# Attention scores of a fused two-model block: one VectorE pass with a row minimum in the first stage, masks added by TensorE in the second and third

## What is computed

```python
s_c = einsum('bghqd,bgnd->bghqn', qblk, k_c) * scale + head_bias(rel_c)      # nsa, compressed keys
s_s = einsum('bghqd,bgqkd->bghqk', qblk, k_sel) * scale + bias_s             # nsa, selected keys
s_w = einsum('bghqd,bgkd->bghqk', qblk, k_wb) * scale + head_bias(rel_w)     # nsa, window
p   = softmax(where(mask, s, NEG))
# even, A: s = q.k * d**-0.5, -inf where a key is not among the 64 best or lies ahead of the query
# odd, C and D: s = q.k * scale, -inf where the key lies ahead of the query; scale is 1/8 for C, 96**-0.5 for D
```

## Time and profile before

| | |
|---|---|
| median of 3 runs | 1409.39 us (1406.6 to 1410.95) |
| the profiled execution | 1416.18 us |
| its span, first to last instruction | 1414.4 us |
| instructions | 27164 |
| mean granted clock of TensorE | 0.972 |
| PE busy | 1311.0 us (93%) |
| DVE busy | 887.8 us (63%) |
| ACT busy | 619.9 us (44%) |
| POOL busy | 430.7 us (30%) |

### The profile page before, as it was taken

The page is one execution under the profiler, slowest core; times in us unless marked ns, Lnnn a source line. Parts: engine busy times, 40 slices in busy tenths (PEclk is TensorE's granted clock), DMA queues, the critical chain, the costliest instruction groups (busy, mean ns, idle before and its releaser), DMA issues.

```text
span 1414.4 us, 27164 instructions
## 1 busy us (share of the span) xinstructions
PE 1311.0 (93%) x10699; PEld 1246.9 (88%) x10717; DVE 887.8 (63%) x1232; ACT 619.9 (44%) x926; POOL 430.7 (30%) x195
## 2 busy tenths in 40 slices
PE   5999999999999998999999789899999997699787
PEld 4999998989999998999999557899998996688667
DVE  3685458786444566555456884755456686774695
ACT  3444335344333345344344774543344445334452
POOL 1444442214444423544430342344441003300042
PEclk9999999999999999999998899999999999999989
DMA  6867764666776546666634113666663461434102
GB/s 195 223 207 223 218 190 133 180 179 190 221 222 184 164 151 185 185 203 191 183 120 149 35 35 105 189 205 185 191 195 105 150 204 43 138 120 137 43 30 90
DMA packets 275098, 222.51 MB, mean 157 GB/s; under 512 B 8082, under 2 KB 256422, under 8 KB 274908
## 3 DMA queue, kind: packets, MB, share of 16 engines
q1 hardware_dynamic: 272528, 215.59, 50.2%
q0 software_dynamic: 1344, 4.46, 1.5%
q10 hardware_dynamic: 1164, 1.62, 0.4%
HBM read 216.40 MB, written 4.19 MB: 156 GB/s over the span
## 4 chain that ended last, share of the span: by engine, by line
PE 74%; DVE 13%; ACT 6%; DMA 3%; issue 3%; POOL 1%; ACTq 0%; POOLq 0%; DVEq 0%; SPq 0%
PE psum L675 23%; PE psum L676 22%; PE psum L677 22%; DVE wal L1587 2%; ACT wah L1170 1%; DVE pbuf L1810 1%; ACT hnh L1239 1%; DVE nmx L1812 1%; DVE hnl L1605 1%; DVE wal L1770 1%; DMA raw_a<-in_ffn_w_in 1%; ACT wbh L1177 1%; PE psum L638 1%; POOL wbl L2197 1%; DVE rms L1577 1%
## 5 line engine op out<-in xcount | busy, mean ns | idle before, releaser
L675 PE MATMUL psum<-hnh,wah 128*128 128x256 f32 (+1 forms) x2080 | 591.6, 284 | 33.5 <-DVE hnl L1605 13.5
L676 PE MATMUL psum<-hnl,wah 128*128 128x256 f32 (+1 forms) x2080 | 582.9, 280 | 0.0
L677 PE MATMUL psum<-hnh,wal 128*128 128x256 f32 (+1 forms) x2080 | 582.6, 280 | 0.0
L2197 POOL TENSOR_TENSOR wbl<-raw_b,wbh 128x1024 fp32r<-128x1024 f32 x111 | 361.3, 3256 | 573.3 <-ACT wbh L1177 467.2
L675 PEld LDWEIGHTS psum<-hnh,wah 128*128 128x128 f32 (+1 forms) x2080 | 397.2, 191 | 21.9 <-issue 10.0
L676 PEld LDWEIGHTS psum<-hnl,wah 128*128 128x128 f32 (+1 forms) x2080 | 395.8, 190 | 2.3 <-issue 1.7
L677 PEld LDWEIGHTS psum<-hnh,wal 128*128 128x128 f32 (+1 forms) x2080 | 395.8, 190 | 0.0
L1587 DVE TENSOR_TENSOR wal<-raw_a,wah 128x2048 fp32r<-128x2048 f32 (+1 forms) x129 | 298.1, 2311 | 102.8 <-ACT wah L1170 101.6
L1170 ACT ACTIVATE wah<-raw_a 128x2048 fp32r<-128x2048 f32 (+2 forms) x127 | 238.9, 1884 | 89.8 <-PE psum L677 64.5
L1277 ACT ACTIVATE gate_hid<-tmp 128x256 f32<-128x256 f32 x88 | 36.7, 417 | 427.9 <-DVE tmp L1705 427.9
L675 PE MATMUL psum<-hidh,wbh 128*128 128x256 f32 x768 | 214.3, 279 | 4.1 <-DVE hidl L1641 3.9
(11 more groups left out here) (289 smaller groups left out, 1557.9 us busy)
## 6 DMA issues: line engine op xcount, KB each, us to landing
raw_a<-in_ffn_w_in SPq DMA_DIRECT2D x176, 512.0 KB, 5.1
raw_b<-in_ffn_w_out SPq DMA_DIRECT2D x88, 512.0 KB, 5.0
raw_a<-in_w_in_even SPq DMA_DIRECT2D x15, 1024.0 KB, 5.4
raw_a<-in_conv_w_in SPq DMA_DIRECT2D x24, 512.0 KB, 3.9
raw_a<-in_w_in_odd SPq DMA_DIRECT2D x11, 1024.0 KB, 5.3
raw_a<-in_w_kv SPq DMA_DIRECT2D x6, 1024.0 KB, 6.4
raw_b<-in_conv_w_out SPq DMA_DIRECT2D x8, 512.0 KB, 5.7
raw_a<-in_attn_w_q SPq DMA_DIRECT2D x4, 1024.0 KB, 5.2
```

What stands on the lines that cost most here:

```text
L675: mm(dst, wh, xh, start=start, stop=False)
L676: mm(dst, wh, xl, start=False, stop=False)
L677: return mm(dst, wl, xh, start=False, stop=stop)
L2197: g.tensor_tensor(wbl[:, s], raw_b[:, s], wbh[:, s].bitcast(F32), ALU.subtract).then_inc(S("b_lo"), 1)
```

## The change

There are five edits.

1. First stage, full duos: instead of L1810, L1812 and L1813, DVE runs four `tensor_tensor_reduce` operations, one for each head and each of the two column ranges. Each adds the bias to the scores from PSUM, multiplies by the negated scale, writes the result to `p` and the row minimum of it to `nmx`. ACT's exponential gets the scale -1. So that the bias can be added ahead of the scale, ACT divides it by the scale when it copies the table to `frow`. The "cmp" duos stay.
2. Second and third stage: PE first writes the mask into both banks, by a bf16 matmul of an identity with the mask (384 columns, `start=True`), and adds the scores to it. DVE takes the two row maxima straight from PSUM and scales them by one small operation; ACT's exponential reads PSUM and applies the scale.
3. Since ACT now reads the banks, PE waits in these stages for `exp_ready` of duo g - 2 instead of `max_ready`, and likewise in the two sums of squares of the third stage.
4. `dmask` leaves the arena for a bf16 tile of its own; `causal16` and `ident16` are bf16 copies that DVE makes in the fourth step of the first FFN, and PE waits for them (`mask_ready`) ahead of the second stage.
5. The last step of the top-64 search adds `causal16` instead of `causal`.

```diff
+        causal16 = sb("causal16", [P, 384], BF16)
+        dmask = sb("dmask", [P, 384], BF16)
+        ident16 = sb("ident16", [P, P], BF16)
...
-        dmask = arena[:, 39:41].rearrange("p a c -> p (a c)")[:, 0:384]
...
                         if g >= 2:
-                            pe.wait_ge(S("max_ready"), g - 1)
-                        if du["kind"] == "full":
+                            pe.wait_ge(S("max_ready" if name == "nsa" else "exp_ready"), g - 1)
+                        if du["bias"] is None:
+                            for i in range(2):
+                                mm(bank[x0 + i][:, 0:384], ident16[:, :], du["mask"][:, :], start=True, stop=False)
+                            for i in range(2):
+                                mm(bank[x0 + i][:, 0:T], q[i][:, P:T], k[i], start=False, stop=False)
+                            for i in range(2):
+                                x = mm(bank[x0 + i][:, T:384], q[i][:, 0:P], k[i][:, 0:P], start=False, stop=True)
+                        elif du["kind"] == "full":
...
+            pe.wait_ge(S("mask_ready"), 1)
             attend("even")
...
-                    pe.wait_ge(S("max_ready"), DBASE["odd"] + 7)
+                    pe.wait_ge(S("exp_ready"), DBASE["odd"] + 7)
...
+                        masked = duos[st]["bias"] is None
                         for m in range(2):
                             r, p = 2 * (g % ND) + m, probs(g)[:, m]
+                            src = bank[2 * (g % 2) + m] if masked else p
                             for lo, hi, i in cuts:
-                                x = act.activation(p[:, lo:hi], p[:, lo:hi], ACT.Exp,
+                                x = act.activation(p[:, lo:hi], src[:, lo:hi], ACT.Exp,
+                                                   scale=duos[st]["scale"] if masked else
+                                                   -1.0 if duos[st]["kind"] == "full" else 1.0,
                                                    bias=nmx[:, r, i:i + 1], accum_out=sm[:, r, i:i + 1])
...
-            act.activation(frow[0:16, 0:EW], bank[7][0:16, 0:EW], ACT.Copy).then_inc(S("bias_copied"), 1)
+            act.activation(frow[0:16, 0:EW], bank[7][0:16, 0:EW], ACT.Copy, scale=1.0 / SQRT_D
+                           ).then_inc(S("bias_copied"), 1)
...
-                        if du["kind"] == "full":
-                            link(v.scalar_tensor_tensor(p, two_banks(x0, P, 384), du["scale"], du["bias"],
-                                                        ALU.mult, ALU.add))
-                            v.reduce_max(nmx[:, r, 1], p[:, :, 0:T], AX, negate=True)
-                            v.reduce_max(nmx[:, r, 0], p[:, :, T:384], AX, negate=True).then_inc(S("max_ready"), 1)
+                        if du["bias"] is None:
+                            v.reduce_max(nmx[:, r, 1], two_banks(x0, P, T), AX, negate=True)
+                            link(v.reduce_max(nmx[:, r, 0], two_banks(x0, P, 384)[:, :, T:384], AX, negate=True))
+                            v.tensor_scalar(nmx[:, r, :], nmx[:, r, :], du["scale"], None, ALU.mult
+                                            ).then_inc(S("max_ready"), 1)
+                        elif du["kind"] == "full":
+                            for i in range(2):
+                                for lo, hi, t in ((0, T, 1), (T, 384, 0)):
+                                    x = v.tensor_tensor_reduce(p[:, i, lo:hi], bank[x0 + i][:, lo:hi],
+                                                               du["bias"][:, i, lo:hi], -du["scale"], 3e38, ALU.add, ALU.min,
+                                                               nmx[:, r.start + i, t:t + 1])
+                            x.then_inc(S("max_ready"), 1)
...
                 v.wait_ge(S("rest_loaded"), 32)
+                v.tensor_copy(ident16[:, :], ident)
+                link(v.tensor_copy(causal16[:, :], causal))
+                v.sem_inc(S("mask_ready"), 1)
                 reduce_angle(angles[0], C_FRB)
```

13 lines of the change are left out of this document (6 added, 7 removed).

## The result

The changed kernel takes 1404.15 us (median of 20 runs, 1394.0 to 1417.6), the kernel before 1411.89 us in its 20 runs beside it (1403.6 to 1423.8). The ratio is 0.9936, 95% interval 0.9912 to 0.9959: faster by 9 us, between 6 and 12. The ratio leaves out one slow run of the changed kernel, 1417.6 us, over 1.5% above its fastest. A second set of 12 runs on another occasion gave 0.9943 (0.9909 to 0.9978). The profiled execution took 1406.93 us, its span was 1405.1.

A forecast was written before the change was run, and what follows sets the result against it. PE bounds the whole program with 74% of the chain; the three attention stages are rings of waits with no engine full. Stage terms -4.2 + 0.4 - 1.3 = -5.1 us take 1409.4 to 1404.3 us, range 1398 to 1413.

The forecast's parts named there:

- Price of the four operations: First stage, DVE: four operations take 1.44 us per full duo instead of 1.91, saving 0.47, between 0.83 saved and 0.68 lost.
- Worth ten, not sixteen: First stage: DVE's pass is in the chain ten times for 16 executions, so the saving counts ten times: -4.7 us.
- that 0.5: First stage: 0.5 us given back where ACT, or PE at low clock, takes over from DVE, leaving -4.2 us.
- Second stage: forecast +0.4: Second stage: PE waits for exponentials, then likely runs at 1.2 GHz; +0.4 us, bounds -0.3 and +1.5.
- Third stage: forecast -1.3: Third stage: C duos gain 1.8 us, the four D duos, bound by PE, lose 0.5; -1.3 us, bounds -3.5 and +3.
- The rest costs nothing: Outside the stages: mask copies, at most 0.8 us, hide in the first FFN's fourth step; other edits cost nothing.
- two signs of being wrong as a whole: Stretches outside the three stages move over 2 us, or a transfer ends the first stage's projection later than its ring.
- C: Third stage: PE at 1.2 GHz in D duos, each costing 2.9 us more; three make +3.6 us, 1413; chance 0.14.
- D: Readouts hidden and D duos at full clock: -8 us in the first stage, -3 in the third, 1399 us; chance 0.20.
- B: First stage: four operations no cheaper than three, giving 0 to -1; sum about -1.5 us, 1408; chance with E 0.24.
- E: Stages: PE and ACT hide DVE, so the change doesn't bring what it says; ends as B; chance with B 0.24.
- A: The forecast itself, all three stages together: -5.1 us, median 1404.3 us, own range 1402 to 1407; chance 0.42.

The follow-up runs named there:

- the filled kernel: Kernel before, with two matmuls of zeros added ahead of the scores of every duo from the sixteenth on in the first stage; ratio 0.9987.
- one pass only: Kernel before with the first stage's edit alone, masks of the second and third stage as before; 1403.9 us against 1417.1, ratio 0.9905.
- masks only: Changed kernel with the first stage put back as before, masks by PE in the second and third; 1409.5 us against 1417.1, ratio 0.9963.
- early low parts: Changed kernel, with POOL making the first two low parts of the first stage's output projection behind its scalings of duos 17 and 20; ratio 0.9962.

## Why the prediction was right, and where it wasn't

**What bounds the kernel, and that DVE's time in the stages is worth time: right.** With the one pass alone and with the masks alone the first and the third stage got shorter where the prediction said.

**Price of the four operations: right in kind, the size off.** The readouts were put at 4 x 0.09 us beside starts of 1.08; they cost nothing that shows, and the set takes 1.11 us, next to the lower bound. With it the prediction's own sum reads 10 x 0.80 - 0.5 = 7.5 us instead of 4.2. DVE's part of the measured 10 us is about 7.

**"Worth ten, not sixteen": near, both ways, for reasons the chain doesn't show.** Of the first twelve full duos ten are on the path when something is added. When 0.80 us each was taken out, the twelve gave 4.5 and 5.6 us (seventh pair at 51.9 and 50.9 us instead of 56.4), some six or seven duos' worth, since ACT lies close behind; with the last four, and without the clock, about 7 us or nine duos' worth. The chain counts who was last, and doesn't tell by how little.

**The clock was all but left out of the first stage.** The prediction weighed it for the second stage and the D duos, as a loss, and in the first only within that 0.5. In the seventh pair and the last stretch it was a gain of some 2.6 to 3.3 us, by the filled kernel. It made the stage -10 instead of -7.

**Is PSUM dearer for DVE? No, as predicted.** The maxima straight from PSUM take 0.69 and 0.41 us in the changed kernel, as from SBUF in the earlier trace rows, and the one pass with a PSUM input 0.41:

```profile
1336.96 0.69 DVE L1824 TENSOR_REDUCE nmx<-psum 128x2 f32<-128x512 f32 x1 [0.73 <-PE psum L877]
1337.57 0.41 DVE L1825 TENSOR_REDUCE nmx<-psum 128x2 f32<-128x256 f32 x1
1338.02 0.17 DVE L1826 TENSOR_SCALAR nmx<-nmx 128x4 f32<-128x4 f32 x1
1338.10 0.17 DVE L1848 RECIPROCAL rs<-sm 128x4 f32<-128x4 f32 x1
```

The small scaling, put at 0.17 to 0.2, adds 0.08 here: the inversion starts at 1338.10.

**"ACT reads PSUM instead of SBUF, nothing": wrong.** It gains 0.17 us a duo. The Trainium skill, "VectorE: DVE Perf Modes", in the same section on the TRN2 errata that the prediction drew on, has ScalarE at 224 cycles ahead of an SBUF source against 172 for PSUM, some 43 ns an operation, an estimate from that page. By that rule, the trace agrees: 1.77 less 1.60 us is 43 ns for each of the four. So the same table's difference between the two sources does not show here for DVE and does for ACT.

**Second stage: forecast +0.4, measured -0.6 to -1.8.** The step that failed is PE's clock after the wait: put at 1.2 GHz, it was at 2.4, as the prediction's other branch ("0.3 earlier than now") had it: the third exponentials start 7.4 us into the stage, 7.8 before. The rest is shorter exponentials and PE's clock later in the stage (0.90 over it and -0.6 us, 1.00 and -1.8, where the kernel before has 0.82); how it splits wasn't measured.

**Third stage: forecast -1.3, measured -3.9 to -4.9.** The third exponential came 9.3 us into the stage (forecast 8.9), since the masks there ran at half clock (0.82 for the pair); where they ran at full it came at 8.4. The C duos are 2.78 apart, forecast 2.8. The step that failed is the D duos' PE work. The prediction put six transposes and a value product behind each D duo's scores, 1.6 us from the earlier trace rows, where PE is busy for all of the 1.62. But PE works three duos back: behind the scores of the first three D duos stand the three transposes of a C duo and the value product of another, and from the first transpose at 1344.42 to the next masks at 1345.55 that takes 1.1 us. A duo needs 2.6 us and not 3.4, as doubling the masks showed. The three steps gave 2.0 us where the forecast lost 0.5.

**"The rest costs nothing", "no transfer holds the end back": nearly.** POOL's low parts now come 2.9 us ahead of the opening matmul instead of 5.2, and the transfers behind them late: PE waits 1.3 to 2.7 us for them, 0.7 before. That is 0.6 us more with the one pass only, and 1.0 and 2.0 in the two traces of the changed kernel. The mask copies were priced at 0.8 at most and hidden. The first of them stood behind POOL's low part (2.19 us instead of some 0.3), and the two made the fourth step of the first FFN 0.65 us longer in all nine traces that have them, of which 0.3 is left at the FFN's end where it keeps the faster pace (147.2 us from there in both traces of the changed kernel, 146.9 in both of before). Of the prediction's two signs of being wrong as a whole the first came: the stretches outside the stages moved by 3 us, more than its 2, though 1.2 of that comes and goes in kernels with and without the change. The second, a transfer that ends the projection later, came in the first trace alone (projection 41.4 us against 39.2).

**Rivals.** C, the slower side, didn't happen in any trace. D, the full prize, is what happened in the stages: readouts hidden, D duos at full clock, -10 and -4. The run time lies above D's 1399 because of what was lost elsewhere and because the kernel before is slower than its first three runs. B and E are out. The mechanism of D came with the number of A, and that is the luck in the number.

## What to carry over

A chain that names an engine ten times doesn't say how far behind the next one is: added time counted on ten of the first twelve duos, removed time only on the worth of six or seven. Where a ring leaves PE idle, shortening any other engine's part can also bring back PE's clock, or lose it, and two throw-away matmuls a step can bring it back as well (8.0 us for 9.5 to 9.7 in one pair, 8.95 for 10.3 in another). When a ring works several places back, price what stands in the queue there, not what will follow: the D duos shared PE with C duos. Once a stage ends sooner, look at what was timed against its old end: here the low parts and transfers of the next projection.

## What the runs showed of the hardware

**Two paces of full-clock matmuls.** With the granted clock at 1.00 throughout, the 256-column matmuls of an FFN follow each other every 113.3 or every 117.8 ns, and an FFN keeps to one pace (the first of the four from about its tenth step on). Scaling steps of the third FFN on DVE, kernel before (8.16 us apart), changed kernel (8.48 apart), 72 matmuls each:

```profile
601.55 0.69 DVE L1705 TENSOR_TENSOR tmp<-psum,rms 128x512 f32<-128x512 f32 x1 [2.88 <-PE psum L677]
609.71 0.69 DVE L1705 TENSOR_TENSOR tmp<-psum,rms 128x512 f32<-128x512 f32 x1 [2.88 <-PE psum L677]
```
```profile
606.14 0.69 DVE L1719 TENSOR_TENSOR tmp<-psum,rms 128x512 f32<-128x512 f32 x1 [3.21 <-PE psum L678]
614.62 0.69 DVE L1719 TENSOR_TENSOR tmp<-psum,rms 128x512 f32<-128x512 f32 x1 [3.21 <-PE psum L678]
```

The kernel before had the slower pace in its second FFN in one trace and in its third in the other, "masks only" had it in three, "early low parts" in none; spans of 1414.4, 1414.8, 1426.3 and 1397.0 us go with that. Each FFN at the slower pace costs 5 to 7 us; of the 56 in the fourteen traces 18 had it. None to three of them in a run is enough for a spread of 20 us, so this is likely the larger part of it, though no kernel was traced often enough to show that. It is why an effect of 0.3% is read from stages and not from one run. What chooses the pace stays open.

**DVE and POOL in each other's way.** A DVE operation with two inputs in SBUF waits for a running POOL subtraction, which has two as well, to its end: 2.39 us for one that takes 0.17. So does a mask copy with one input: 2.19 us, where the next copy, three times as wide, takes 0.35. Beside POOL's scaling, with one tensor input, the 128x4 multiplication takes its 0.17. A POOL scaling that meets a DVE subtraction waits in turn (2.57 us a pair for 1.91).

**Small things.** An accumulator read behind the one-pass operation costs no time on the engine that shows (0.08 us, alongside the next operation). A pair of 384-column bf16 matmuls costs 0.34 us at full clock. The versions with the one pass in the third stage and with DVE's low parts or filling come to 1402.7 and 1405.0 us (ratios 0.990 and 0.991); they beat the kernel before, and by their four stretches (160 and 159 us, changed kernel 165 and 161) the changed one too, but their intervals overlap with its and with that of "one pass only" (0.9905), so by time alone that isn't shown.
